# State matrices and output tables of a state-space layer lend each other free slots, and gate rows are made ahead of the last unit of the gate stage

## The reference, cut to what matters

```python
bu = einsum('btgs,gps->btgp', u_chunk, b_bar)          # input into the states
_, xs = lax.associative_scan(_ssm_combine, (a, bu))    # x[t] = lam_bar * x[t-1] + bu[t]
xs = xs + powers[None] * h[:, None]
y = einsum('btgp,gsp->btgs', xs, cmat).real            # output from the states
```

## Time and profile before

| | |
|---|---|
| median of 3 runs | 1661.11 us |
| lowest and highest | 1659.18 and 1666.45 us |
| the profiled execution, its own time | 1659.68 us |
| its span, first to last instruction | 1657.9 us |
| TensorE busy | 1572.6 us, 95% of the span |
| VectorE, ScalarE, GpSimd busy | 44%, 22%, 8% |
| mean granted TensorE clock | 0.990 |
| moved by DMA | 270.80 MB, mean 163 GB/s |

### The profile page before, as it was taken

How to read it: one execution, slowest core, us unless ns; L and a number is a source line. 1 busy time by engine, 2 the same in 40 slices (tenths; PEclk the granted TensorE clock), 3 DMA queues, 4 the chain that set the end, 5 groups by cost and what they waited for, 6 DMA issues and landing times.

```text
span 1657.9 us, 24080 instructions
## 1 busy us (share of the span) xinstructions
PE 1572.6 (95%) x9932; PEld 1058.1 (64%) x9932; DVE 727.8 (44%) x1541; ACT 370.0 (22%) x874; POOL 140.0 (8%) x232
## 2 busy tenths in 40 slices
PE   4999989999999998999888999999999989999999
PEld 3455556666655577668777888874445554788843
DVE  5889845555589784883660000103202212233300
ACT  1222333333212223213321000000114441311100
POOL 4013420000023122000010000000000000000000
PEclk9999999999999999999999999999999999999999
DMA  9845760410785456567672444454542123444431
GB/s 317 224 165 191 253 218 1 124 43 1 267 258 186 160 184 242 194 228 263 237 268 72 152 153 152 150 177 154 178 152 102 51 102 102 153 152 153 152 140 64
DMA packets 171189, 270.80 MB, mean 163 GB/s; under 512 B 51021, under 2 KB 84920, under 8 KB 169800
## 3 DMA queue, kind: packets, MB, share of 16 engines
q1 hardware_dynamic: 145840, 201.08, 35.9%
q0 software_dynamic: 16512, 42.49, 8.0%
q10 hardware_dynamic: 8728, 25.69, 4.1%
HBM read 226.16 MB, written 42.99 MB: 162 GB/s over the span
## 4 chain that ended last, share of the span: by engine, by line
PE 81%; issue 13%; DMA 2%; DVE 2%; POOL 1%; ACT 1%; POOLq 0%; DVEq 0%; ACTq 0%
PE bank L434 76%; PE bank L437 4%; DMA memory<-in_w_mod 1%; POOL memory L2362 1%; DMA k_scratch<-memory 1%; DMA memory<-in_s_log_dt 0%; DVE memory L2245 0%; POOL k_scratch L2347 0%; ACT memory L1181 0%; ACT memory L1565 0%; DMA memory<-mc_scratch 0%; ACT memory L1309 0%; DVE memory L1929 0%; DVE memory L1637 0%; DVE memory L1962 0%
## 5 line engine op out<-in xcount | busy, mean ns | idle before, releaser
L434 PE MATMUL bank<-memory 128*128 128x256 f32 (+9 forms) x9104 | 1481.9, 368 | 61.5 <-issue 12.6
L434 PEld LDWEIGHTS bank<-memory 128*128 128x128 f32 (+4 forms) x9104 | 963.4, 160 | 536.2 <-issue 386.8
L437 PEld LDWEIGHTS bank<-memory 128*128 128x128 f32 (+1 forms) x828 | 96.3, 143 | 58.9 <-issue 36.1
L437 PE MATMUL bank<-memory 128*128 128x128 f32 (+1 forms) x828 | 111.8, 279 | 19.9 <-ACT memory L1153 8.7
L2347 POOL DMA_DIRECT2D k_scratch<-memory x128 | 76.2, 630 | 14.3 <-ACT memory L1226 13.8
L2341 POOL DMA_DIRECT2D mc_scratch<-memory x32 | 28.0, 874 | 505.9 <-DVE memory L1847 447.7
L2275 DVE SCALAR_TENSOR_TENSOR memory<-bank,memory 128x255 f32<-128x255 f32 x44 | 21.0, 478 | 104.6 <-ACT memory L1591 104.6
L2173 DVE TENSOR_SCALAR memory<-bank,memory 128x256 f32<-128x256 f32 x16 | 6.6, 477 | 122.8 <-PE bank L434 122.8
L1962 DVE TENSOR_REDUCE memory<-bank 128x1 f32<-128x512 f32 (+1 forms) x48 | 30.2, 684 | 61.9 <-PE bank L434 61.9
L2124 DVE TENSOR_TENSOR memory<-memory 128x256 f32<-128x256 f32 x56 | 23.2, 414 | 77.1 <-ACT memory L1403 77.1
L1309 ACT ACTIVATE memory<-bank,memory 128x512 f32<-128x512 f32 (+1 forms) x64 | 36.3, 579 | 85.5 <-DVE memory L1965 85.5
(11 more groups left out here) (254 smaller groups left out, 960.4 us busy)
## 6 DMA issues: line engine op xcount, KB each, us to landing
memory<-in_s_w_glu SPq DMA_DIRECT2D x16, 2048.0 KB, 7.5
memory<-in_w_mod SPq DMA_DIRECT2D x12, 2048.0 KB, 14.0
memory<-in_w_ffn_up SPq DMA_DIRECT2D x22, 1024.0 KB, 6.7
memory<-in_w_in SPq DMA_DIRECT2D x10, 2048.0 KB, 7.9
mc_scratch<-memory POOLq DMA_DIRECT2D x32, 512.0 KB, 4.5
mb_scratch<-memory ACTq DMA_DIRECT2D x32, 512.0 KB, 3.7
memory<-mb_scratch SPq DMA_DIRECT2D x32, 512.0 KB, 5.5
memory<-mc_scratch POOLq DMA_DIRECT2D x32, 512.0 KB, 6.1
```

Source lines behind the costliest of these rows:

```text
L434: return nc.tensor.matmul(o, l, r, start=start, stop=stop, skip_group_check=free)
L437: return nc.tensor.transpose(o, i, ident[0:n, 0:n])
```

## The change

The three slots of the state matrices and the three of the output tables become six that both can use. `mb_slot(u)` puts the matrices of the units 6, 7, 8, 12, 13 and 14 into the slots 4, 5, 3, 4, 5, 3, which are those of the output tables, not yet in use then. `mc_slot(u)` puts the tables of the units 27, 28 and 29 into the slots of the state matrices, which are done by then, so that the tables 30 and 31 find their slots free after the units 24 and 25. The waits follow. The SP order changes in three places, and the first three tables now wait for the units 14, 12 and 13. In the gate stage `mod_turned`, `mod_columns` and `gate_rows` move ahead of unit 15 on TensorE, DVE and ACT.

```diff
+        def mb_slot(u):
+            return 3 + (u + 1) % 3 if u in (6, 7, 8, 12, 13, 14) else u % 3
+        def mb_user(u):
+            return max((v for v in range(u) if mb_slot(v) == mb_slot(u)), default=None)
+        def mc_slot(u):
+            return u - NU + 8 if NU - 5 <= u < NU - 2 else u % 3
...
 # TensorE, end of the gate stage (ACT: gate_rows(0) ahead of unit_stored(15))
+            mod_turned(0, 5, 7)
+            gate_rows(0)
             unit_turned(15)
-            mod_turned(0, 5, 7)
             for i in range(2):
                 pe.wait_ge(*S.at("qnT", i))
-            gate_rows(0)
...
 # DVE
             unit(14)
+            mod_columns(0, 5)
             unit(15)
...
             V.tensor_copy(krT, at_bank("krT")).then_inc(*S.up("krT"))
-            mod_columns(0, 5)
...
             def mc_load(u0, u1):
                 for u in range(u0, u1):
-                    if u >= 3:
-                        pool.wait_ge(*S.at("yc_mm", u - 3))
+                    if u < 3:
+                        pool.wait_ge(*S.at("st_mm", (14, 12, 13)[u]))
+                    elif mc_slot(u) >= 3:
+                        pool.wait_ge(*S.at("st_mm", NU - 1))
+                    else:
+                        pool.wait_ge(*S.at("yc_mm", u - 3 if u < NU - 2 else u - 6))
...
             def mb_load(u0, u1):
                 for u in range(u0, u1):
-                    if u >= 3:
-                        sp.wait_ge(*S.at("st_mm", u - 3))
+                    if mb_user(u) is not None:
+                        sp.wait_ge(*S.at("st_mm", mb_user(u)))
...
-            mb_load(0, 3)
+            mb_load(0, 6)
+            sp.wait_ge(*S.at("x1_scaled", 1))
+            mb_load(6, 8)
             t_load(0, 0)
-            mb_load(3, 8)
+            for kp in (14, 15):
+                sp.wait_ge(*S.at("k_out%d" % (kp % 2), kp))
+            mb_load(8, 9)
             ring(("s5u", 2))
+            mb_load(9, 12)
             ring(("s5u", 3))
-            mb_load(8, 11)
+            mb_load(12, 15)
             t_load(0, 1)
-            mb_load(11, 19)
+            mb_load(15, 19)
...
             t_load(2, 0)
+            t_load(2, 1)
+            mb_load(27, 30)
             ring_load(first_glu)
-            t_load(2, 1)
-            mb_load(27, 32)
+            mb_load(30, 32)
             t_load(3, 0)
```

More of the change, by code:

```diff
@@ L280, in build, with mb_, mc_tab @@
         powR = gtb[:, 1, :]
+        def mb_slot(u):
+            return 3 + (u + 1) % 3 if u in (6, 7, 8, 12, 13, 14) else u % 3
+        def mb_(u):
+            i = mb_slot(u)
+            return mb_in[:, i, :] if i < 3 else mc_in[:, i - 3, :]
+        def mb_user(u):
+            return max((v for v in range(u) if mb_slot(v) == mb_slot(u)), default=None)
+        def mc_slot(u):
+            return u - NU + 8 if NU - 5 <= u < NU - 2 else u % 3
+        def mc_tab(u):
+            i = mc_slot(u)
+            return mc_in[:, i, :] if i < 3 else mb_in[:, i - 3, :]
         def u_(b, par, g):
@@ L797, in additions @@
                     pe.wait_ge(*S.at("u_t", (q, g // 2)))
-                    pe.wait_ge(*S.at("mb_in%d" % (u % 3), u))
+                    pe.wait_ge(*S.at("mb_in%d" % mb_slot(u), u))
                     b = bank(pe, ("st", u), [("xs", u)], next(spare))
@@ L803, in additions @@
                             c = dr * 512 + (ql * 2 + ri) * P + 64 * par
-                            last = mm(b[64 * par:64 * par + 64, n * NC:(n + 1) * NC], mb_in[:, u % 3, c:c + 64], u_(q, par, ql * 8 + g),
+                            last = mm(b[64 * par:64 * par + 64, n * NC:(n + 1) * NC], mb_(u)[:, c:c + 64], u_(q, par, ql * 8 + g),
                                       n == 0, n == 7, True)
@@ L825, in outputs @@
                     pe.wait_ge(*S.at("states", q))
-                    pe.wait_ge(*S.at("mc_in%d" % (u % 3), u))
+                    pe.wait_ge(*S.at("mc_in%d" % mc_slot(u), u))
                     for dr in range(2):
@@ L837, in outputs @@
                                     c = (dr * 4 + ql * 2 + ri) * P
-                                    last = mm(banks[4 + 2 * hq + par][m:m + 32, i * P:(i + 1) * P], st, mc_in[r, u % 3, c:c + P],
+                                    last = mm(banks[4 + 2 * hq + par][m:m + 32, i * P:(i + 1) * P], st, mc_tab(u)[r, c:c + P],
                                               False, i == 3 and dr == 1 and ri == 1, True)
```

4 lines of the change are left out of this document (2 added, 2 removed).

## The result

| | before | after |
|---|---|---|
| median of 4 runs each | 1661.34 us | 1647.35 us |
| lowest and highest | 1659.18 and 1666.45 us | 1644.85 and 1649.25 us |
| ratio, 95% interval | | 0.9913 [0.9891, 0.9935] |
| the profiled execution, its own time | 1659.68 us | 1648.27 us |
| its span | 1657.9 us | 1646.5 us |

What follows compares the result with a forecast made beforehand. TensorE, busy 1572.6 of 1657.9 us, bounds the kernel, leaving only idle and half-clock time to win. Terms 1.2 + 5.8 + 5.0 + 9.5 + 0.4 = 21.9 us gave 1637.8 us profiled, 1639 us median; range 1632 to 1650 us.

Steps and rivals of the forecast that it cites:

- Unit 3: S5 layer: its matrix is asked for ahead of 1 MB of direct kernels, its wait goes; gain 1.2 us.
- Quarter 1: Unit 8 to the end of `direct(0, 1)`: earlier loads cut 16.16 us to 10.4; gain 5.8 us.
- Unit 15 follows 1.3 later, at 8.4: Quarter 1: unit 15's matrix lands 1.3 us behind the direct kernels, 8.4 us after unit 8's start; 1.4 us wait.
- Quarter 3: Units 24 to 29: the 2 MB block goes behind unit 29, unit 27's wait shrinks; gain 5.0 us.
- Of that I give back 0.9: Quarter 3: units 30 and 31, now behind the 2 MB block, cost 0.9 of 5.9 us.
- The bound of 2.0: Quarter 3's poor end: gain only 2.0 us if unit 30's and 31's matrices land as late as the slow ones.
- Tail: Outputs of unit 24 to first product after the last transposes: earlier tables save 8.5 us, clock 1.0; gain 9.5 us.
- I counted half the clock: Tail: GLU work at half clock would give back 2 us; half of it, 1.0 us, was counted.
- Gate stage: Ahead of the first head: TensorE's wait for DVE's unit 15 moves behind the gate rows, staying 3.8 us; gain 0.4 us.
- the loads' rival: Quarters 1 and 3: DMA engines are the bound, loads come back as other waits; gain 10.7 us, 1650 us, chance 0.10.

Runs made afterwards that it cites:

- the kernel with the earlier transpose: Kernel after, with `mod_turned(0, 5, 7)` moved into the loop over the gate's tiles, between tiles 14 and 15: 1642.46 us, ratio 0.9886.
- the kernel with all three moves: Kernel after, with modulation transpose earlier, direct kernels (0, 1) ahead of unit 14's matrix, GLU block behind unit 31's: 1637.62 us, second run 1635.1 us.
- the kernel with `direct(0, 1)` later: Kernel after, earlier transpose, GLU block behind unit 31; matrices 14 and 15 before direct kernels, `direct(0, 1)` behind `u_tile(2, 0)`: 1638.43 us, ratio 0.9861.

## Why the prediction was nearly right, and what failed in it

- **Unit 3.** Forecast 1.2 us, measured 1.2 and 1.0 us. Right.
- **Quarter 1.** Forecast 5.8 us, measured 2.8 and 2.5 us up to unit 24; on the stretch that was forecast, up to `u_tile(2, 0)`, 3.5 and 2.6 us (16.16 less 12.63 and 13.47). The step that failed is "Unit 15 follows 1.3 later, at 8.4". It landed 9.5 us after the start of unit 8 (705.31 - 695.77), 2.5 us behind the direct kernels. The earlier trace rows gave a sign of it: the direct kernels of before landed at 693.6 + 4.9 = 698.5 us and the first matrix behind them at 696.5 + 4.7 = 701.2, 2.7 us later, which I had not compared, though there the matrix was asked for 2.9 us behind them and here 0.5 us. The step of 1.3 us was also short by its own sum, 5.2 - 4.7 + 0.93 = 1.43. The wait became 2.88 us in place of 1.4, and a stretch of 3.41 us at half clock came back behind it, which I had taken as saved. With the order of the two loads turned the stretch took 10.06 us, the forecast's 10.4 nearly; in the three profiles with the direct kernels ahead of unit 14 it took 10.1, 11.8 and 11.1 us, the last two with 2.7 and 2.0 us of stalls inside units.
- **Quarter 3.** Forecast 5.0 us, measured 0.4 and 2.3 us. The first half held in the main: 4.1 to 4.2 of 5.9 us. In the first profile the missing 1.8 us are unit 27's wait of 1.16 us and the units 27 to 29, which took 3.66 us in place of 3.0. The step that failed is "Of that I give back 0.9": the units 30 and 31 behind the 2 MB block gave back 3.6 and 2.0 us. I had set the wait of unit 30 at 0.5 us; it was 1.66 and 1.57, and in the first profile a half-clock stretch followed it. The bound of 2.0 rested on just this case and was the better value, though the first profile lies below it: the earlier trace rows showed a matrix behind that same block. Shown by one line in the kernel after (10.32 us for 13.96 and 12.30) and in the kernel before (4.6 us won with no new slot).
- **Tail.** Forecast 9.5 us with the clock, measured 8.0 and 9.6 us (7.7 + 0.3, 7.7 + 2.0), and 9.7 us in the kernel with the tables alone. The size was right; of the 0.9 us by which the stretch is longer than the 12.6 us forecast, 0.7 us is a stall inside a unit that no step had. I counted half the clock; it is all or nothing from one execution to the next.
- **Gate stage.** Forecast 0.4 us, measured -0.8 us twice, +0.4 and -0.8 us with that part alone, and 1.0007 [0.9995, 1.0019] in time. The mechanism was right, the wait and its place to 0.1 us (3.73 for 3.8). What I had not priced is that the half-clock stretch there grew from 3.41 us to 6.83 us (214.85 to 221.68).
- **Unforeseen.** 1.7 us near 600 us, in work the change doesn't touch.

Of the rivals, that of the loads (1650 us) was nearest in size, but not by its mechanism. It held the DMA engines to be the bound. The trace has their share at 0.99 from unit 24 to `direct(2, 1)`, yet putting one block later won 1.7 to 3.6 us in the kernel after and 4.6 us in the kernel before. It is the order within the full queue that counts. The Trainium skill ("DMA: Bandwidth & Descriptors", section "Issuing engines are not separate DMA queues") says that transfers of all issuers interleave on the same 16 engines. The trace agrees that they share them: from 710 to 712 us of the trace after, packets of SP's queue take 61.0% of the 16 engines and those of POOL's 39.9%. What decided here is within one issuer: the matrix of unit 30 landed 1.3 us behind a block asked for 5.6 us ahead of it. That the median lies within the range (1647.35 in 1632 to 1650) is in part luck: the upper end stood for the loads' rival, and two terms were off by 3.0 and 4.6 us.

## What to carry to other kernels

More slots let a load be asked for earlier; when it lands depends also on what has been asked for just before it (unit 15's matrix: 7.4 us behind the direct kernels, 5.6 us with unit 14's matrix just ahead). So for each load follow the queue and put a large block that is needed late behind every small one needed soon; that one move of a 2 MB block won 4.6 us of a stretch in the old kernel, with no slot added. And when a wait is to be removed on one engine, look first for the small operation that the late engine waits for: here a single transpose, done one tile earlier, took the wait from 3.73 to 0.64 us, where moving whole steps past each other won nothing.

## What the runs showed of the hardware

**A short wait costs clock in some executions.** The same work behind the same wait ran at full clock in one execution and for 3.41 us at half clock in another. In the trace after and, below it, in that of before (the columns are those of TensorE's timeline):

```profile
599.68 8.81 PE L451 MATMUL bank<-memory 128*64 128x256 f32 x64 [2.11 <-ACT memory L1198]
```

```profile
599.72 7.13 PE L434 MATMUL bank<-memory 128*64 128x256 f32 x64 [2.12 <-ACT memory L1181]
```

The wait is 2.11 and 2.12 us, the work 1.68 us longer. It came in both profiles of the kernel after, both of the gate part alone, and in three more; it stayed away in before and six others. It is not the program alone, since the kernel with the earlier transpose and the kernel with all three moves are the same up to there and differ by 1.7 us. The Trainium skill ("TensorE: Matmul & The Clock Gate", section "HAM oscillation — how this bites in real kernels") prices a throttled stretch at half its length, 1.7 us here, and the trace agrees (8.81 - 7.13 = 1.68). What decides in one execution was not settled. For reading, it means that two profiles of this kernel differ by 2.2 us (1648.27 and 1646.03) with nearly equal waits, and stretches have to be compared, not totals.

**Stalls in the middle of a unit.** At 859.86 us of the trace after (above) TensorE has stood still for 0.71 us after 34 records, which is 2 records into unit 29, where no semaphore is waited for. The six profiles with the tables in shared slots and the GLU block ahead of unit 31 have 0.60 to 0.77 us there. The kernel with all three moves has 1.87 and 0.80 us in quarter 1, its second run 1.49 and 0.53, each time after the same 105 and 231 records; the kernel with `direct(0, 1)` later has 1.23 us after 231. These places are 126 records apart, and each has a weight load beside it. The DMA queues of the second run of the three moves show from 694 to 695 us, among the others (kind, packets, MB, share):

```profile
q8 instruction: 1, 0.02, 5.7%
```

and one more from 698 to 699 us. The trace has these packets at 16 KB each, from 694.47 us for 0.91 us and from 698.82 for 1.11. The stalls end at 696.75 and 701.17, 1.4 and 1.2 us behind them. In all eleven stalls named here the stall ended 1.2 to 1.5 us after such a packet (858.38 and 859.86 us in the trace after). The queue has 80 packets in one execution, for 19 864 matmuls and weight loads (page of the kernel before), which is 248 to a packet; between the two places in quarter 1 lie 126 matmul records and as many weight loads, 252 in all.

The same places also run without a stall, and there the packet was early. In none of the fourteen profiles does the record behind the 105 start less than 1.2 us after the packet's end. The kernel with `direct(0, 1)` later has the packet 1.7 us ahead of it and no stall; the three moves have it late and stall. That packet starts at most 0.7 us after unit 8 does in nine profiles, all with idle DMA engines in the microsecond before it, and 2.5 to 3.0 us after in the other five, all with a DMA share of 0.86 or more there.

So these stalls look like waits for the program's own instructions, held back where other transfers fill the DMA engines. That is read from times that agree; no run took the traffic away and left the rest alone, so it isn't shown. It is also rare: of the 186 such packets from 640 to 880 us of the fourteen profiles with a DMA share of 0.9 or more around them, eleven were followed by one of these stalls. If it holds, a full set of DMA engines cost TensorE up to 2.7 us in a stretch of 12 (all three moves) even with all its data there.
